# The end of a hybrid decoder kernel: final weighting and scaling divided among VectorE, ScalarE and GpSimd in another way

## The reference, cut to what matters

```python
h = rms_norm(x, norm_g);  z = h @ w_in          # (520, 2048) x (2048, 6144)
pm = pool_mix(u, ...);    a = dilated_attention(q, k, v, ...)
x = x + concat([pm * silu(gp), a * silu(ga)]) @ w_out      # w_out: 2048 x 2048

def rms_norm(x, g):                              # the final norm: y = rms_norm(x, final_norm_g)
    y = x * rsqrt(mean(x * x, axis=-1) + 1e-6)
    return y * g
```

## Time and profile before

| | before |
|---|---|
| median of three runs | 822.56 us |
| lowest, highest | 821.51, 828.95 us |
| the profiled execution | 821.09 us |
| its span, first to last instruction | 819.3 us |
| TensorE busy | 807.1 us, 99% |
| VectorE busy | 627.4 us, 77% |
| ScalarE busy | 398.9 us, 49% |
| GpSimd busy | 203.2 us, 25% |
| bytes moved by DMA | 150.04 MB |
| mean granted TensorE clock | 0.996 of full speed |

### The profile page before, as it was taken

One profiled execution on the slowest core, in us unless ns is written; L12 is line 12 of the kernel. 1 busy time (PEld: TensorE's weight loads), 2 busy tenths in 40 slices (PEclk: granted clock), 3 DMA queues, 4 the chain that ended last, 5 costly groups with the idle time before them and its releaser, 6 DMA issues.

```text
span 819.3 us, 17483 instructions
## 1 busy us (share of the span) xinstructions
PE 807.1 (99%) x6625; PEld 802.6 (98%) x6625; DVE 627.4 (77%) x1347; ACT 398.9 (49%) x875; POOL 203.2 (25%) x340
## 2 busy tenths in 40 slices
PE   9999999999999999999999999999999999999995
PEld 8999999999999999999999999999999999999994
DVE  4657895897589778958885897689888886777765
ACT  4745435533554454345435533553465345555554
POOL 2103502520360045014402610450000131222220
PEclk9999999999999999999999999999999999999998
DMA  8569647856774696578558756884668567766565
GB/s 297 142 173 232 168 125 171 231 144 168 188 208 122 163 233 169 152 175 228 152 141 186 204 147 182 193 214 123 172 195 272 156 181 203 207 184 174 150 180 218
DMA packets 271499, 150.04 MB, mean 183 GB/s; under 512 B 44448, under 2 KB 261472, under 8 KB 271392
## 3 DMA queue, kind: packets, MB, share of 16 engines
q1 hardware_dynamic: 239784, 118.97, 53.7%
q0 software_dynamic: 12672, 20.59, 9.9%
q10 hardware_dynamic: 18960, 9.38, 4.0%
HBM read 119.49 MB, written 28.27 MB: 180 GB/s over the span
## 4 chain that ended last, share of the span: by engine, by line
PE 87%; DVE 6%; DMA 3%; issue 1%; ACT 1%; SPq 1%; POOL 1%; DVEq 0%; ACTq 0%
PE pj L889 64%; PE pj L1048 13%; PE ps_s L946 1%; PE ps_s L948 1%; PE ps_o L977 1%; PE ps_o L975 1%; DMA out<-arena 1%; PE ps_o L889 1%; DVE w_lo L1624 1%; PE ps_t L995 1%; PE ps_s L995 1%; PE ps_s L889 1%; PE ps_s L827 1%; DVE arena L1755 1%; DMA w_raw<-in_w_out 0%
## 5 line engine op out<-in xcount | busy, mean ns | idle before, releaser
L889 PE MATMUL pj<-mov_hi,w_hi 128*128 128x260 f32 (+1 forms) x1632 | 332.1, 285 | 0.3 <-DVE mov_lo L1645 0.3
L889 PE MATMUL pj<-mov_hi,w_lo 128*128 128x260 f32 (+1 forms) x1632 | 328.3, 283 | 0.0
L889 PE MATMUL pj<-mov_lo,w_hi 128*128 128x260 f32 (+1 forms) x1632 | 327.8, 282 | 0.0
L889 PEld LDWEIGHTS pj<-mov_hi,w_hi 128*128 128x128 f32 x1632 | 252.7, 189 | 2.1 <-issue 0.6
L889 PEld LDWEIGHTS pj<-mov_lo,w_hi 128*128 128x128 f32 x1632 | 251.4, 188 | 0.0
L889 PEld LDWEIGHTS pj<-mov_hi,w_lo 128*128 128x128 f32 x1632 | 251.4, 188 | 0.0
L1148 ACT ACTIVATE w_hi<-w_raw 128x640 fp32r<-128x640 f32 (+1 forms) x157 | 121.4, 773 | 228.5 <-PE pj L889 159.3
L1624 DVE TENSOR_TENSOR w_lo<-w_raw,w_hi 128x640 fp32r<-128x640 f32 (+1 forms) x157 | 135.5, 863 | 62.7 <-ACT w_hi L1148 62.3
L1566 POOL DMA_DIRECT2D p_scratch<-extra x168 | 104.8, 631 | 82.4 <-DVE extra L1727 79.9
L1597 POOL DMA_DIRECT2D y_scratch<-arena x56 | 37.6, 678 | 110.5 <-DVE arena L2209 81.3
L1540 POOL DMA_DIRECT2D out<-arena x8 | 4.6, 569 | 213.0 <-DMA arena<-arena 213.0
(11 more groups left out here) (275 smaller groups left out, 1295.3 us busy)
## 6 DMA issues: line engine op xcount, KB each, us to landing
w_raw<-in_w_in SPq DMA_DIRECT2D x96, 320.0 KB, 4.1
w_raw<-in_w_in SPq DMA_DIRECT2D x48, 384.0 KB, 4.5
arena<-in_cache_k_win SPq DMA_DIRECT2D x16, 384.0 KB
arena<-in_cache_v_win SPq DMA_DIRECT2D x16, 384.0 KB
p_scratch<-extra POOLq DMA_DIRECT2D x112, 48.0 KB, 3.3
w_raw<-in_w_out SPq DMA_DIRECT2D x26, 192.0 KB, 3.0
arena<-in_cache_k_win SPq DMA_DIRECT2D x8, 512.0 KB
arena<-in_cache_v_win SPq DMA_DIRECT2D x8, 512.0 KB
```

What stands on the lines that cost most here:

```text
L889: mm = pe.matmul(dst[h][:, 0:own.stop - own.start], w, m[:, k, own], start=(k == 0 and i == 0), stop=(c == 2 and k == KT - 1 and i == 2))
```

## The change

- VectorE no longer weights tile 13, scales no row group 2, and no longer handles the last two tiles of row groups 2 and 3 and the samples. Row groups 0 and 1 it treats as before, except that it waits until tile 13 is weighted ahead of scaling.
- GpSimd, after its last DMAs, weights tile 13 for all rows, then tiles 14 and 15 for row groups 2 and 3 and the samples, then multiplies row group 2 (three pieces) and the samples (2048 columns in one) by `rstd`, all with TENSOR_TENSOR, the second operand repeated by a zero stride.
- ScalarE scales row group 3 alone, in three pieces that now reach to column 2047. The first stands where all stood, the second between row group 0's square root and its scaling, the third behind row group 0's scaling and a wait for tiles 14 and 15. It no longer scales the samples.
- SP's stores stand in another order: 3, 2, 3, 2 (the first two pieces of row groups 3 and 2), all four of row group 0, the third pieces of 3 and 2, the samples, and three of row group 1.

```diff
--- before.py
+++ after.py
@@ -787,28 +787,35 @@
                     sp.wait_ge(y_scaled, e - 2)
                     load_res(e)
 
-            for i, (lo, hi) in enumerate(zip(Y_AT, Y_AT[1:])):
-                last = i == len(Y_AT) - 2
-                sp.wait_ge(f_out, 4 if last else i + 1)
-                sp.dma_start(yp[:, 2, lo:hi], y[:, 2, lo:hi]).then_inc(f_st, 16)
-                sp.wait_ge(f_out_a, i + 1)
-                if last:
-                    sp.wait_ge(f_out, 5)
-                sp.dma_start(yp[:, 3, lo:hi], y[:, 3, lo:hi]).then_inc(f_st, 16)
-            for b in range(2):
-                if b == 1:
-                    sp.wait_ge(f_out_s, 1)
-                    sp.wait_ge(f_out_a, 6)
-                    sp.dma_start(ys_out, y_s[0:NB, :]).then_inc(f_st, 16)
-                for i in ((0, 2, 1, 3), (0, 1, 3))[b]:
-                    lo, hi = ROW_AT[i], D_MODEL if i == 3 else ROW_AT[i + 1]
-                    if i < 2:
-                        sp.wait_ge(f_out, 5 + 3 * b + i + 1)
-                    else:
-                        sp.wait_ge(f_out_a, 3 + 3 * b + i - 1)
-                    if i == 3:
-                        sp.wait_ge(f_out, 5 + 3 * b + 3)
-                    sp.dma_start(yp[:, b, lo:hi], y[:, b, lo:hi]).then_inc(f_st, 16)
+            def store_rows(t, i):
+
+                lo, hi = Y_AT[i:i + 2]
+                sp.wait_ge(*((f_out_s, i + 1) if t == 2 else (f_out_a, (1, 2, 5)[i])))
+                sp.dma_start(yp[:, t, lo:hi], y[:, t, lo:hi]).then_inc(f_st, 16)
+
+            def store_piece(b, i):
+
+                lo, hi = ROW_AT[i], D_MODEL if i == 3 else ROW_AT[i + 1]
+                if i < 2:
+                    sp.wait_ge(f_out, 3 * b + i + 1)
+                else:
+                    sp.wait_ge(f_out_a, 2 + 3 * b + i - 1)
+                if i == 3:
+                    sp.wait_ge(f_out, 3 * b + 3)
+                sp.dma_start(yp[:, b, lo:hi], y[:, b, lo:hi]).then_inc(f_st, 16)
+
+            store_rows(3, 0)
+            store_rows(2, 0)
+            store_rows(3, 1)
+            store_rows(2, 1)
+            for i in (0, 1, 2, 3):
+                store_piece(0, i)
+            store_rows(3, 2)
+            store_rows(2, 2)
+            sp.wait_ge(f_out_s, 4)
+            sp.dma_start(ys_out, y_s[0:NB, :]).then_inc(f_st, 16)
+            for i in (0, 1, 3):
+                store_piece(1, i)
             sp.wait_ge(f_st, 16 * (2 * (len(Y_AT) - 1) + 1 + 2 * (len(ROW_AT) - 1)))
             for s, n in ((kv_st, KV_ST // 16 * PAIRS), (kn_st, PAIRS), (vn_st, PAIRS),
                          (us_st, SQS * PAIRS), (up_st, SQS * PAIRS), (hist_st, 1),
@@ -1496,9 +1503,15 @@
             act.wait_ge(ms_done, 1 + 1)
             act.activation(sd[:, 2:5], ms[:, 2:5], ACT.Sqrt).then_inc(sd_done, 1)
             act.wait_ge(rs_done, 4 + 4)
-            for lo, hi in zip(Y_AT, Y_AT[1:-1] + (LAST,)):
+
+            def scale_rows(i):
+                lo, hi = Y_AT[i:i + 2]
+                if i == 2:
+                    act.wait_ge(y_scaled, KT - 1)
                 act.activation(y[:, 3, lo:hi], y[:, 3, lo:hi], ACT.Copy,
                                scale=rstd[:, 3:4]).then_inc(f_out_a, 1)
+
+            scale_rows(0)
             for b in range(2):
                 act.wait_ge(half_added, 3 + 2 * b)
                 act.wait_ge(half_sq, 1 + b)
@@ -1506,15 +1519,17 @@
                                accum_out=ss_y[:, b, KT - 2:KT - 1]).then_inc(half_sq, 1)
                 act.wait_ge(ms_done, 1 + 2 + b)
                 act.activation(sd[:, b:b + 1], ms[:, b:b + 1], ACT.Sqrt).then_inc(sd_done, 1)
+                if b == 0:
+                    scale_rows(1)
                 act.wait_ge(rs_done, 4 + 8 + 4 * b)
+                act.wait_ge(y_scaled, KT - 2)
                 for lo, hi in zip(ROW_AT[2:], ROW_AT[3:]):
                     act.activation(y[:, b, lo:hi], y[:, b, lo:hi], ACT.Copy,
                                    scale=rstd[:, b:b + 1]).then_inc(f_out_a, 1)
                 if b == 0:
-                    act.activation(y_s[0:NB, 0:LAST], y_s[0:NB, 0:LAST], ACT.Copy,
-                                   scale=rstd[0:NB, QT:QT + 1]).then_inc(f_out_a, 1)
+                    scale_rows(2)
             lo, hi = ROW_AT[2:4]
-            act.wait_ge(f_out_a, 7)
+            act.wait_ge(f_out_a, 6)
             act.dma_start(yp[:, 1, lo:hi], y[:, 1, lo:hi]).then_inc(f_st, 16)
 
 
@@ -1599,6 +1614,30 @@
 
             for d in range(KT - 2):
                 send_tile(d)
+
+            def weigh(rows, smp, d):
+
+                gf = x_res[d % 3][:, SEQ + P:SEQ + 2 * P]
+                n = rows.shape[1]
+                pool.tensor_tensor(rows, rows, gf.unsqueeze(1).to_broadcast([P, n, P]), ALU.mult)
+                return pool.tensor_tensor(smp, smp, gf[0:NB, :], ALU.mult)
+
+            tiles = [slice(P * d, P * d + P) for d in range(KT)]
+            pool.wait_ge(y_squared, 5 * (KT - 2))
+            weigh(y[:, :, tiles[KT - 3]], y_s[0:NB, tiles[KT - 3]], KT - 3).then_inc(y_scaled, 1)
+            pool.wait_ge(half_sq, 1)
+            pool.wait_ge(half_sq_v, 1)
+            weigh(y[:, 2:4, tiles[KT - 2]], y_s[0:NB, tiles[KT - 2]], KT - 2)
+            weigh(y[:, 2:4, tiles[KT - 1]], y_s[0:NB, tiles[KT - 1]], KT - 1).then_inc(y_scaled, 1)
+            pool.wait_ge(rs_done, 4 + 4)
+            pool.wait_ge(y_scaled, KT - 1)
+            for lo, hi in zip(Y_AT, Y_AT[1:]):
+                pool.tensor_tensor(y[:, 2, lo:hi], y[:, 2, lo:hi],
+                                   rstd[:, 2:3].to_broadcast([P, hi - lo]),
+                                   ALU.mult).then_inc(f_out_s, 1)
+            pool.tensor_tensor(y_s[0:NB, :], y_s[0:NB, :],
+                               rstd[0:NB, QT:QT + 1].to_broadcast([NB, D_MODEL]),
+                               ALU.mult).then_inc(f_out_s, 1)
 
 
         @block.vector
@@ -2363,19 +2402,13 @@
             half_add(KT - 2)
             half_add(KT - 1)
             half_square()
-            scale_y(KT - 3)
             root(0, slice(2, 5))
-            for lo, hi in zip(Y_AT, Y_AT[1:-1] + (LAST,)):
-                dve.tensor_scalar(y[:, 2, lo:hi], y[:, 2, lo:hi], rstd[:, 2:3], None,
-                                  ALU.mult).then_inc(f_out, 1)
-            for t in (2, 3):
-                scale_last(y[:, t, :], P, rstd[:, t:t + 1]).then_inc(f_out, 1)
-            scale_last(y_s[0:NB, :], NB, rstd[0:NB, QT:QT + 1]).then_inc(f_out_s, 1)
             for b in range(2):
                 row_add(b, KT - 2)
                 row_add(b, KT - 1)
                 row_square(b)
                 root(1 + b, slice(b, b + 1))
+                dve.wait_ge(y_scaled, KT - 2)
                 for lo, hi in zip(ROW_AT, ROW_AT[1:3]):
                     dve.tensor_scalar(y[:, b, lo:hi], y[:, b, lo:hi], rstd[:, b:b + 1], None,
                                       ALU.mult).then_inc(f_out, 1)
```

## The result

| | before | after | after, a second time |
|---|---|---|---|
| median of the runs | 822.99 us (11 runs) | 830.85 us (11 runs) | 828.43 us (10 runs) |
| lowest, highest | 821.47, 828.95 | 827.13, 835.64 | 825.79, 833.58 |
| ratio to the kernel before, 95% interval | | 1.0084 [1.0062, 1.0107] | 1.0050 [1.0021, 1.0078] |
| span of the profiled execution | 819.3 us | 829.0 us | 823.9 us |
| TensorE's last matmul ends | 809.03 | 813.86 | 809.07 |

The change costs 0.5 to 0.8%, where 0.2% was to be won. 821.0 us was forecast, and the range ended at 827.0. TensorE ends where it does in before, to 0.04 us, so that the times can be laid beside the earlier trace rows as they stand.

The account below looks back on a forecast made before the run. Only the tail could move, bound by VectorE and DMA: 3.75 MB without a hole from 807.2 to 816.8, plus 0.97, ends at 817.7. That takes 1.6 off 822.56, giving 821.0 us; own range 819.6 to 821.9, whole range 819.6 to 827.0.

Parts of the forecast that it names:

- What bounds the kernel: Only the 10.3 us tail and 7 us of VectorE work beside TensorE's last matmuls can move; VectorE, then DMA, bound it.
- the transfer bound: Stores at the end: 4.27 MB at 390 GB/s take 10.9 us, so 1.3 of VectorE's 2.9 us gained are lost.
- VectorE loses work: VectorE near the end: row group 0 added at 803.72, scaled from 806.28; VectorE ends at 812.8, 2.9 us earlier.
- GpSimd gains work: GpSimd's added work at 1.69 ns a column plus 0.18 us each; row group 2 ready by 808.4, samples at 812.0.
- rival C: GpSimd slower than its squares, delaying samples and stores; at 3.4 ns a column the span ends near 825.4; chance 12%.
- rival A: GpSimd and VectorE lock each other out, stalling row group 0's root steps; end 823.5, 4.2 us slower; chance 27%.
- slower by over 1%: Whole kernel: a measurable slowdown of over about 8 us, reached only by rival C's far end with other mishaps; chance 2%.
- Rival B: The lock touches only long VectorE instructions (row_square, the two-fold tensor_scalar); 0.4 us faster than before; chance 12%.
- Rival D: The change does nothing because something else holds row group 0 or 1; span 819.3 us; chance 4%.

Follow-up runs that it names:

- after_again: The changed kernel, unchanged, run a second time later; ratio to before 1.0050, 14.8 us from TensorE's last matmul to the end.
- b3: b1 with ScalarE's scaling of the samples cut in two halves, the first before row group 0's square; ratio to before 0.9993.
- x2: The kernel before plus two unused GpSimd multiplications of 2048 columns on the idle weight buffer; ratio to before 1.0074.
- b1: The kernel before with only tile 13's weighting moved to GpSimd; ratio to before 1.0014.
- x3: The kernel before plus four unused GpSimd memsets of 2048 columns, which write and read nothing; ratio to before 1.0064.
- x4: The kernel before plus ten unused GpSimd multiplications of one column; ratio to before 0.9986.
- x1: The changed kernel with the samples scaled by one ScalarE instruction instead of GpSimd; ratio to before 1.0011.
- x5: x1 with GpSimd scaling row group 2 in 16 instructions of 128 columns instead of three; ratio to before 1.0022.
- x7: The changed kernel with the one-column Newton steps of row groups 0 and 1 written as TENSOR_SCALAR; ratio to before 1.0035.

## Why the prediction was wrong

*What bounds the kernel: right.* Only the tail moves with the change. TensorE's end is at 809.07 in after_again. Whether the transfer bound that the forecast drew would have held was not tested: in after_again the flow stood for 3.8 us, and b3's end, which did not move, came with a gap in the flow.

*VectorE loses work: right, and not what counts.* The weighting of tile 13 and the pieces of row group 2 and the last tiles are gone, and row group 0 is added at once behind the first root (805.02).

*GpSimd gains work: nearly right.* Forecast 1.04 us for 512 columns of tile 13, 0.61 for 256 and 0.39 for eight rows: 1.28, 0.73 and 0.45, so 2.15 ns a column between the first two. That is over the 2 ns that rival C was to show, but worth 0.2 us at most in one instruction. Group 2's three pieces: 3.99 forecast, 3.94 measured. The samples: 3.64 forecast, 3.59 to 3.74 measured. Rival C (3.4 ns a column) is out. The Trainium skill's 4497 ns for 2048 columns (GPSIMD Engine Reference, Elementwise — side-by-side cycle accounting) is 0.8 to 0.9 us too long for this case; x2's two, on 128 partitions, took 3.98 and 3.59, the first with a wait for VectorE in it.

*The step that failed* is the one that let VectorE's small instructions keep the lengths of the earlier trace rows beside GpSimd ("From reduce to scaling is 1.41 us", taken from before, for the durations; "The forecast has 45%, A 27%" for the choice). The text had all the parts of rival A. It left the choice to two overlaps of 0.06 and 0.12 us, which could not decide it. What each instruction on the way to row group 0's scaling took over its length in before:

| instruction | in before | in after_again | late |
|---|---|---|---|
| first root, scaling of 128x3 | 0.17 | 0.57 | 0.40 |
| first root, Newton steps 1 and 2 | 0.16, 0.16 | 0.61, 0.39 | 0.68 |
| row_square | 0.29 | 0.71 | 0.42 |
| row group 0's steps 2 and 3 | 0.16, 0.16 | 1.60, 3.52 | 4.80 |
| sum | | | 6.30 |

The forecast had the scaling at 806.28, and it came at 812.61, 6.33 us late. The table comes near that, though not term by term. The root's end was 1.30 late (its 1.08 of the table, 0.16 of a longer half square and 0.18 of a gap behind it, less a start 0.13 earlier than in before). Row group 0's reduce added 0.20, since the forecast had 0.25 us of waiting for ScalarE where row_square stood. The rest is 4.83. From the scaling to the end the forecast had 817.7 - 806.28 = 11.4 us, and it took 823.9 - 812.61 = 11.3. This agreement is luck: the forecast had a transfer without a hole and VectorE waiting for TensorE in it, and what ran was 5.2 us of VectorE and 6.1 us of stores behind its end. The tail was forecast at 8.7 us and was 14.8. Against before it lost 4.6 us: VectorE ended 2.1 later, and 2.5 came behind its end, where the new order holds back the third pieces (the table of the experiments; rival A had these bytes in its 3.09 MB, the forecast counted on a row group 0 in time).

*Rival A, with its numbers.* It had the root at 813.3 (812.57), group 0's first store at 813.8 (813.09), the hole in the DMA rates near 809 to 814 (810.2 to 814.0), and the end at 823.5 (823.9). So mechanism and size were on record as the second choice. Two sizes in it were off and nearly cancelled. The root came 0.7 us earlier, for A's sum 804.95 + 7.6 + 0.8 has 0.8 us behind the samples for which no row stands. And the stretch from the first store to the end took 10.8 instead of 9.7 us. This second one is a term that neither case had. SP needs 1.09 us for the samples' store and 3.32 for the last three, against 0.30 and 1.45 in before, so its last store is out at 820.7, 2.9 us behind VectorE's end at 817.8; in before it was 0.5 us behind. In b3, b1, x2, x3 and x4, with the old order of the stores, the last three took 1.4 to 1.5 us again; in x1, x5 and x7, with the new order, 3.3 to 3.4 us. So it goes with the new order, in which row group 0 and the two 448 KB stores leave in one block just ahead of the last ones; what in it makes the issue slow was not taken apart.

*The range* missed by 3.9 us for the first comparison and by 1.4 for the second. The tail explains 4.6 us of the difference to before: 823.9 - 819.3. The ratios are worth 4.1 us (1.0050) and 6.9 us (1.0084), so one agrees with the tail and the other is 2.3 us above it. The early stall of TensorE is 4.8 us in the execution that has it, and would fill that gap if about half more of the runs of after had it; that stays open. That the case "slower by over 1%" was given 2% holds: neither ratio reaches 1.01, though the first one's interval does.

*Rival B* (only long instructions lock) is out, since three-column instructions of 0.16 us waited. *Rival D* is out by the ratios.

## What to carry to other kernels

Ahead of moving work from VectorE to GpSimd, list what VectorE does beside it, and price each instruction with two SBUF inputs, and each TENSOR_SCALAR wider than a column, at the rest of GpSimd's current instruction and not at its own length; a chain of small steps pays once for every GpSimd instruction that it meets. Put work on GpSimd where VectorE has only reduces, PSUM adds or nothing (b1's tile 13 cost 0.16 us that way), and give long rows on few partitions to ScalarE, where 2048 columns took 1.98 us (x1) and no VectorE instruction beside them was stretched; x1's reduce for row group 1 waited 0.45 us for ScalarE instead of 0.24. When work changes engines, lay the new order of the stores beside the bytes: a late group at the head of the queue holds back what stands behind it (here argued from the bytes, 0.92 MB or 2.4 us). Where a rule speaks against a change and the rows can't refute it, its case should be the forecast, unless its price is small.

## What the runs showed of the hardware that I had not expected

- Width decides for TENSOR_SCALAR: with three columns it stood behind a memset or a TENSOR_TENSOR (0.94 and 3.42 instead of 0.17 us), with one column it kept its 0.15 to 0.21 us beside a TENSOR_TENSOR. The Trainium skill (VectorE: DVE Perf Modes, Mode 2×_2P — use both read ports for one tensor) ties the use of both ports to the outermost non-unit dimension being even, or odd and equal in source and destination. Three columns fit that and a single column has no such dimension; the runs agree.
- A second SBUF input counts even if it is the first one again: row_square, with both inputs the same tile, took 0.71 and 0.81 us instead of 0.29. An add of PSUM and SBUF did not wait (0.49 us for two beside GpSimd in after_again, 0.47 in before).
- SP's issue of a store grew from 0.30 to 1.09 us and from 0.39 to 1.52 us where many stores were under way. No run here isolates why.
